# Final outputs of a one-core trunk: 32x32 turns on VectorE and 128-byte stores from three queues, in place of TensorE turns

## What is computed

```python
def fox_layer(x, q_pos, f_q, k, v, f_k, k_pos, norm_g, w_in, q_norm_g, w_out, blocked):
    ...
    y = (o * jax.nn.silu(z)) @ w_out
    return x + y.astype(x.dtype)
# y_prompt: (1, 256, 2048), y_sample: (1, 32, 2048)
```

## Time and profile before

| | us |
|---|---|
| median of 3 runs | 1652.79 (1652.4 to 1653.79) |
| the profiled execution | 1653.42 |
| its span | 1651.6 |
| TensorE busy (PE) | 1632.0, 99% |
| VectorE busy (DVE) | 1091.3, 66% |
| ScalarE busy (ACT) | 782.2, 47% |
| GpSimd busy (POOL) | 279.2, 17% |

### The profile page before, as it was taken

How to read it: one execution, slowest core, us unless ns; L and a number is a source line. 1 busy time by engine, 2 the same in 40 slices (tenths; PEclk the granted TensorE clock), 3 DMA queues, 4 the chain that set the end, 5 groups by cost and what they waited for, 6 DMA issues and landing times.

```text
span 1651.6 us, 29367 instructions
## 1 busy us (share of the span) xinstructions
PE 1632.0 (99%) x11683; PEld 1563.8 (95%) x11683; DVE 1091.3 (66%) x2089; ACT 782.2 (47%) x1306; POOL 279.2 (17%) x536
## 2 busy tenths in 40 slices
PE   7999999999989999999999999999999999999999
PEld 6999999999979999999999989999999999999998
DVE  5976666766567877768677788655535545653755
ACT  5545344443454453535435445545443555445442
POOL 1210111011234232321322311022102000000000
PEclk9999999999999999999999999999999999999999
DMA  7576667666876676666756655465668554555533
GB/s 193 176 195 166 184 185 205 165 183 185 228 197 209 198 245 182 209 211 198 243 175 215 195 190 165 134 220 173 192 199 283 157 171 141 181 171 168 155 115 110
DMA packets 296505, 308.23 MB, mean 187 GB/s; under 512 B 58792, under 2 KB 274624, under 8 KB 296368
## 3 DMA queue, kind: packets, MB, share of 16 engines
q1 hardware_dynamic: 269648, 225.82, 46.6%
q0 software_dynamic: 26064, 79.70, 14.1%
q10 hardware_dynamic: 656, 0.82, 0.3%
HBM read 259.49 MB, written 46.79 MB: 185 GB/s over the span
## 4 chain that ended last, share of the span: by engine, by line
PE 93%; DVE 2%; DMA 2%; ACT 1%; issue 1%; SPq 1%; POOL 0%; ACTq 0%; DVEq 0%
PE acc L178 26%; PE acc L180 25%; PE acc L179 25%; PE aux L1510 3%; PE aux L1357 2%; PE aux L1483 2%; PE aux L1336 1%; PE aux L2770 1%; DMA x_tok<-in_x_prompt 1%; PE aux L1517 1%; PE aux L2164 1%; PE aux L1529 1%; DMA a_row<-decay_scratch 1%; DVE w_lo L158 1%; PE aux L1464 0%
## 5 line engine op out<-in xcount | busy, mean ns | idle before, releaser
L158 DVE TENSOR_TENSOR w_lo<-raw,w_hi 128x1024 fp32r<-128x1024 f32 x400 | 485.1, 1219 | 294.1 <-ACT w_hi L153 292.3
L153 ACT ACTIVATE w_hi<-raw 128x1024 fp32r<-128x1024 f32 x400 | 414.6, 1056 | 196.3 <-PE acc L180 169.6
L178 PE MATMUL acc<-xg_hi,w_hi 128*128 128x304 f32 x1536 | 470.7, 306 | 3.7 <-DVE w_lo L158 3.4
L180 PE MATMUL acc<-xg_hi,w_lo 128*128 128x304 f32 x1536 | 463.7, 302 | 0.0
L179 PE MATMUL acc<-xg_lo,w_hi 128*128 128x304 f32 x1536 | 462.5, 301 | 0.0
L178 PEld LDWEIGHTS acc<-xg_hi,w_hi 128*128 128x128 f32 x1536 | 289.2, 188 | 8.1 <-issue 5.0
L179 PEld LDWEIGHTS acc<-xg_lo,w_hi 128*128 128x128 f32 x1536 | 290.0, 189 | 0.8
L180 PEld LDWEIGHTS acc<-xg_hi,w_lo 128*128 128x128 f32 x1536 | 289.3, 188 | 0.0
L105 POOL TENSOR_TENSOR cell<-cell 1x1 f32<-1x1 f32 x151 | 73.0, 483 | 1102.5 <-DVE xc_lo L899 318.7
L178 PE MATMUL acc<-xb_hi,w_hi 128*128 128x288 f32 x512 | 156.3, 305 | 0.2 <-DVE w_lo L158 0.2
L178 PE MATMUL acc<-hz_hi,w_hi 128*128 128x304 f32 x512 | 155.1, 303 | 0.4 <-DVE zs L983 0.4
(11 more groups left out here) (492 smaller groups left out, 2916.4 us busy)
## 6 DMA issues: line engine op xcount, KB each, us to landing
raw<-in_a_w_in SPq DMA_DIRECT2D x128, 512.0 KB, 4.0
raw<-in_a_w_out SPq DMA_DIRECT2D x64, 512.0 KB, 4.4
raw<-in_w_kvf SPq DMA_DIRECT2D x64, 512.0 KB, 4.4
raw<-in_b_w_in SPq DMA_DIRECT2D x64, 512.0 KB, 4.0
raw<-in_b_w_out SPq DMA_DIRECT2D x32, 512.0 KB, 3.5
raw<-in_a_wq SPq DMA_DIRECT2D x16, 512.0 KB, 4.1
raw<-in_a_wk SPq DMA_DIRECT2D x16, 512.0 KB, 4.0
raw<-in_a_wv SPq DMA_DIRECT2D x16, 512.0 KB, 5.3
```

The lines of the kernel that those rows point to most:

```text
L153: act.activation(w_hi[:, s, :, :], raw[:, s, :, :], ACT.Copy).then_inc(hi_made, 1)
L158: dve.tensor_tensor(w_lo[:, s, :, :], raw[:, s, :, :], w_hi[:, s, :, :].bitcast(F32), ALU.subtract).then_inc(lo_made, 1)
L178: pe.matmul(acc[b][:, 0:width], wh, x_hi[:, k0 + k, :], start=st, stop=False)
L180: mm = pe.matmul(acc[b][:, 0:width], wl, x_hi[:, k0 + k, :], start=False, stop=last and k == 3)
```

## The change

The four events y0 to y3, their 48 transposes on TensorE, the copies by ACT and VectorE and the buffer y_tok go. In each of the last eight steps VectorE, having added the two tiles, turns each of them (128x288) in blocks of 32x32 into y_blk[128, 16, 288]. After that, row i of a quarter of 32 partitions holds, for each block of 32 tokens, the 32 channels of that quarter at token i: a run of 128 bytes of the output. Each step's slice of 256 channels is stored by 12 transfers: eight of y_prompt (two tiles by four quarters, 256 runs each) and four of y_sample (four quarters, 64 runs each). SP, ACT and POOL issue four of them each; POOL's are two of y_prompt and two of y_sample. All three wait for the semaphore blk_made, which now counts 8 more. On SP the stores stand behind all loads. On ACT those of slice j-1 stand in step j behind that step's w_hi. On POOL they stand at its end. SP waits for its own and ACT's 64 transfers at the end, POOL for its own 32.

```diff
+        y_blk = sb("y_blk", [P, KD, TQ], F32, p5)
+        Y_PARTS = (((0, (0, 1, 2)), (3, (0,))), ((1, (0, 1, 2)), (3, (1,))), ((2, (0, 1, 2)), (3, (2,))))
-        for k, slot in enumerate(order[first:]):
-            slot[5].extend((LAST_G, e) for e in Y_OUT.get(k, "").split())
...
+        def y_store(eng, j, share, stored):
+            eng.wait_ge(blk_made, BLK_Y + j + 1)
+            for a, parts in Y_PARTS[share]:
+                rows_ = slice(32 * a, 32 * a + 32)
+                for part in parts:
+                    if part < 2:
+                        c = P * (2 * j + part) + 32 * a
+                        eng.dma_start(o["y_prompt"][0, :, c:c + 32].rearrange("(b i) c -> i b c", i=32),
+                                      y_blk[rows_, 2 * j + part, 0:SEQ].rearrange("i (b c) -> i b c", c=32))\
+                           .then_inc(stored, 16)
+                    else:
+                        eng.dma_start(o["y_sample"][0].rearrange("i (k a j) -> a i k j", a=4, j=32)[a][:, 2 * j:2 * j + 2, :],
+                                      y_blk[rows_, 2 * j:2 * j + 2, SEQ:TQ]).then_inc(stored, 16)
...
@@ fox_sync @@
-            for c in range(4):
-                cut = slice(c * 512, (c + 1) * 512)
...
-                    freed(sp, use(LAST_G, f"y{c}", t))
-                    src = y_tok[:, t, cut] if t < 2 else y_tok[P - DEC:P, t, cut]
-                    sp.dma_start(dst, src).then_inc(y_stored, 16)
-            sp.wait_ge(y_stored, 16 * 12)
+            for j in range(8):
+                y_store(sp, j, 0, y_stored)
+            sp.wait_ge(y_stored, 16 * 8 * 8)
...
@@ fox_gpsimd, at its end @@
+            for j in range(8):
+                y_store(pool, j, 2, v_out)
+            pool.wait_ge(v_out, 80 * (GROUPS - 1) + 16 * 4 * 8)
...
@@ fox_scalar, in the loop over the steps, behind high_part; and once at its end @@
+                if (kind, g) == ("OUT", LAST_G) and j:
+                    y_store(act, j - 1, 1, y_stored)
...
+            y_store(act, 7, 1, y_stored)
...
@@ fox_vector, behind add_out @@
+            def turn_y(j, tile):
+                for m in range(2):
+                    u = tile + m
+                    wait(dve, acc_free[u.turn(4)], u.rounds(4) + 1)
+                    ins = dve.transpose(y_blk[:, 2 * j + m, :], xT[:, 2 * j + m, META:T])
+                ins.then_inc(blk_made, 1)
...
@@ fox_tensor @@
-            def turn_y(c):
...
-                        mm = pe.transpose(bank[:, k * P:(k + 1) * P], xT[:, 4 * c + k, META + t0:META + t0 + P],
-                                          ident[:, :])
```

More of the change, by code:

```diff
@@ L356, in trunk @@
         BLK_STORES = (16 * 24, 16 * 8)
+        BLK_Y = 2 * HEADS
         USES, TURNED, STATES = 15, 3, 7
@@ L2281, in trunk @@
         oe_hi, oe_lo = sb("oe_hi", [P, GRP, TQ], F32R, p5), sb("oe_lo", [P, GRP, TQ], F32R, p5)
-        y_tok = sb("y_tok", [P, 3, D], F32, p5)
+        y_blk = sb("y_blk", [P, KD, TQ], F32, p5)
+        pad_y = sb("pad_y", [P, 3 * D - KD * TQ], F32, p5)
         p5.close()
@@ L2304, in trunk @@
         PARTS_LAST = {9: "H0", 11: "H1", 13: "H2", 15: "H3"}
-        Y_OUT = {2: "y0", 4: "y1", 6: "y2", 7: "y3"}
+        Y_PARTS = (((0, (0, 1, 2)), (3, (0,))), ((1, (0, 1, 2)), (3, (1,))), ((2, (0, 1, 2)), (3, (2,))))
         order, at = [], A_FOX
@@ L2330, in trunk @@
                     slot[5].extend((g, e) for e in PARTS_LAST.get(k, "").split())
-        first = len(order)
         at = add("OUT", LAST_G)
-        for k, slot in enumerate(order[first:]):
-            slot[5].extend((LAST_G, e) for e in Y_OUT.get(k, "").split())
         assert len(order) == 24 * GROUPS
@@ L2343, in trunk @@
                 USE[g, e] = uses
-                uses += {"q": 3, "b": 3, "K": 1, "X": 1, "Y": 2, "T": 2 if e != "TY" else 1, "O": 1, "y": 3}.get(e[0], 0)
+                uses += {"q": 3, "b": 3, "K": 1, "X": 1, "Y": 2, "T": 2 if e != "TY" else 1, "O": 1}.get(e[0], 0)
         def use(g, e, k=0):
@@ L2362, in fox_sync @@
                     store_values(sp, Count(GROUPS - 1), last_out)
-            for c in range(4):
-                cut = slice(c * 512, (c + 1) * 512)
-                for t, dst in enumerate((o["y_prompt"][0, 0:P, cut], o["y_prompt"][0, P:256, cut],
-                                         o["y_sample"][0, :, cut])):
-                    freed(sp, use(LAST_G, f"y{c}", t))
-                    src = y_tok[:, t, cut] if t < 2 else y_tok[P - DEC:P, t, cut]
-                    sp.dma_start(dst, src).then_inc(y_stored, 16)
-            sp.wait_ge(y_stored, 16 * 12)
+            for j in range(8):
+                y_store(sp, j, 0, y_stored)
+            sp.wait_ge(y_stored, 16 * 8 * 8)
         def fox_gpsimd(pool):
@@ L2500, in high_oz @@
                 act.activation(hi[:, m, :], zg[:, m, :], ACT.Copy).then_inc(oz_hi_made, 1)
[L2502 to L2507, removed]
             def event(g, e):
@@ L2529, in event @@
                     high_oz(g, int(e[1]))
-                elif e[0] == "y":
-                    take_y(int(e[1]))
             for n, kind, g, j, tile, events in order:
@@ L2722, in fox_vector @@
                     add_out(n, j, tile)
+                    if g == LAST_G:
+                        turn_y(j, tile)
                 for e in events:
@@ L2834, in outputs @@
                           skip_group_check=True).then_inc(use_ready, 1)
-            def turn_y(c):
[L2837 to L2842, removed]
-                        mm = pe.transpose(bank[:, k * P:(k + 1) * P], xT[:, 4 * c + k, META + t0:META + t0 + P],
-                                          ident[:, :])
-                        if k == 3:
-                            mm.then_inc(use_ready, 1)
             def event(g, e):
@@ L2866, in event @@
                     outputs(g, int(e[1]))
-                elif e[0] == "y":
-                    turn_y(int(e[1]))
             for n, kind, g, j, tile, events in order:
```

## The result

The changed kernel is slower, by about a quarter of a percent. Over twelve runs of each, the ratio of its time to the time before is 1.0027, with a 95% interval of 1.0018 to 1.0036; the medians are 1655.45 us (1651.94 to 1658.25) and 1650.56 us (1647.67 to 1653.79). That is 4 to 5 us where 2.3 us less was forecast. The profiled execution took 1655.83 us, its span is 1654.0.

A forecast was written before the change was run, and what follows sets the result against it. PE was taken as the bound, busy 1632.0 of 1651.6 us. The last slice's first issue 4.1 us earlier, less 1.3 for POOL's issues and 0.5 for its landing, gave -2.3 us, 1650.5 from 1652.79; range 1649.0 to 1653.6.

The forecast's parts named there:

- The PE part: TensorE, last OUT: three turns between products go, 1.29 us each, 3.9 us in all; last add starts at 1642.4.
- The VectorE part: VectorE, last OUT: sixteen new turns of 0.44 us; w_lo, adds and turns take 2.8 us of a 3.20 us step.
- the room of 3.5 us: ACT's stores delay the making of w_hi and w_lo, but PE wants w_lo 3.5 us later, so it costs nothing.
- The queues: Four issues a slice: SP and ACT 2.0 us, POOL 2.6 to 3.1, under 3.20; POOL's last issue gives back 1.3 us.
- The landings: End of the last stores: POOL's take 2.6 us to land, 0.5 more than the 2.1 of y's stores before.
- The transfers: A slice of 2304 pieces of 128 bytes moves in 1.6 us, half a step, hidden for seven slices.
- What ACT and POOL hold up: Work behind the new waits: ACT's and SP's delays cost nothing, and nothing of the kernel stands behind POOL's wait.
- the term that the sum carried over from SP: Kernel's end: 2.58 us from SP's last issue to the span's end, taken as 3.1 for POOL's last issue.
- The slower side: Slower by over 3.3 us, from the backlog and part of ACT's stall; chance 0.11.
- a backlog on POOL: POOL's four issues exceed 3.20 us a slice and delay accumulates; at 1.2 us an issue, +11 us; chance 0.08.
- a stall by ACT: ACT's issues hold back w_hi, or VectorE w_lo, and PE waits: +1 to +4 us; chance 0.04.
- The first rival: SP and ACT end last, POOL being as quick: -3.5 to -2.6 us, 1649.3 to 1650.2; chance 0.24.

The follow-up runs named there:

- e1: Changed kernel with POOL storing nothing in the last OUT, SP and ACT issuing six stores each a slice; ratio to the kernel before 0.9991.
- e8: Changed kernel, stores and waits untouched, but the block left without the drain instruction at the end of POOL's program; ratio to the kernel before 0.9982.
- e5: As e1, but POOL's last act is a wait for all stores of SP and ACT; ratio to the kernel before 1.0033.
- v2: Changed kernel with POOL storing its share of slices 0 to 5 only, and the last slice added, turned and stored in two halves; ratio to before 0.9973.
- e3: Changed kernel with POOL storing its share of slices 0 to 3 only, SP and ACT taking it afterwards; ratio to before 0.9980, again 0.9978.
- e4: Kernel before, with the last of its twelve stores (y_sample, 64 KB) issued by POOL instead of SP; ratio to before 1.0045.
- e2: Changed kernel, but SP instead of POOL waits for POOL's transfers at the end; ratio to the kernel before 1.0005.
- e6: Changed kernel with two 1x1 multiplications on POOL behind its wait for its landings; ratio to the kernel before 1.0033.

## Why the prediction was wrong

It forecast -2.3 us, and +4 to +5 came; 1655.45 us lie outside the range that it gave (1649.0 to 1653.6).

- **The PE part** (3 x 1.29 = 3.9 us, last add 22.4 us after the first) was right: 26.26 became 22.40.
- **The VectorE part** was right. A turn takes 0.45 us (0.44 forecast), add and pair of turns 1.57 (1.6). PE never waits for w_lo in these steps; VectorE waited for w_hi once, 0.7 us, because ACT made it behind its issues; that moved one add by 0.2 us, and PE, for which the room of 3.5 us was reckoned, not at all.
- **The queues** were close. SP's last issue starts 2.95 us after the last add (forecast 3.15). POOL was cheaper than its nearest rows: 0.59 us for a y_prompt part, where 0.76 was taken, and 0.54 for a y_sample part; its last issue starts 3.6 us after the last add (forecast 3.8). There was no backlog at the end, 2.2 us a slice against 3.20.
- **The landings** were as forecast or better: 2.3 to 2.4 us by POOL in the median, where 2.6 was taken.
- **The transfers** of 128 bytes stayed hidden, as e1 and e8 show; a loss of rate at small pieces costs nothing that these runs show.
- **The step that failed** stands in "What ACT and POOL hold up": "Behind POOL's wait is nothing of the kernel." Behind it is the drain at the end of POOL's program, 6.36 us in the changed kernel. With it goes the term that the sum carried over from SP, 2.58 us from the last issue to the end, made 3.1 for POOL's landing: for POOL's last transfer that stretch measured 8.9 us (1645.05 to 1654.0), 2.2 until POOL sees the landing and 6.7 until the end. The trace of the kernel before could have told: its line L2888 has POOL's drain with 10.9 us, ended 120 us ahead of the end, and so hidden.
- **The rivals.** The slower side was given 0.11, to a backlog on POOL and a stall by ACT. The first named the right queue and the wrong mechanism: the backlog wants more than 3.45 us a slice, and 2.2 were taken. The first rival, that SP and ACT end last, POOL being as quick, is nearest to what the change does once the drain is out: e8 gains 31.6 - 28.5 = 3.1 us, between its -3.5 and -2.6.

So the change without the drain gains 3.1 us (31.6 - 28.5), the exposed drain costs 6.4 (34.9 - 28.5), and what is left is +3.3 from first add to end; the interval of the ratio (3.0 to 5.9 us) holds it.

## What to carry to other kernels

Before an engine is given work near the end of a program, ask what its program still has to do behind that work. Neither its timeline nor its busy time shows it: it stands among the instructions of the line that closes the block, and when it is exposed, in the waits of another engine at that line. An engine whose last work lies far ahead of the end hides the price of its leaving, but the row is there already: POOL's drain, 10.9 us. What it will cost when it is late is measured by one run in which that engine does nothing but wait at the end (e5). Compare tails from a common event rather than by spans, when executions differ by more upstream than the change moves.

## What the runs showed of the hardware

- POOL's drain at the close of the block takes 5.7 (v2) to 7.5 us (e3), and 10.9 where it begins beside POOL's last loads (before). From POOL's last act to the end of the span are 6.1 to 7.1 us, whether that act is a landing (6.7 in the changed kernel, 6.1 in v2, 7.1 in e4), an issue (6.6, e2), a small product (6.6, e6) or a wait for others' transfers (7.1, e5); without the drain SP waits 0.3 us (e8).
- Stores of 256 pieces of 128 bytes cost POOL 0.59 us to issue, less than its transfers of 256 rows of 2 KB (out_p_k, 0.76), and land in 2.4 us in the median, where SP's and ACT's take 2.1 and 2.3:

```profile
out_y_prompt<-y_blk ACTq DMA_DIRECT2D x24, 32.0 KB, 2.3
out_y_prompt<-y_blk SPq DMA_DIRECT2D x24, 32.0 KB, 2.1
...
out_y_prompt<-y_blk POOLq DMA_DIRECT2D x16, 32.0 KB, 2.4
```

- SP and ACT, each issuing such a store every 0.49 us, moved 21071 packets, 20008 of them under 512 bytes, between 1618 and 1651 us (e1), and PE's steps stayed at 3.20 us on average, though VectorE's adds were up to 4.65 us apart.
